# Last expert block turned inside the down product in front, and the sampled tokens' tile taken first in the final combination

## The reference, cut to what matters

```python
h = x + mix
# every token goes to the top 2 of 32 experts; assignments are sorted by expert, padded to blocks of 128 rows
def expert_block(args):
    e, tok = args
    xb = x_pad[tok]
    hmid = jax.nn.silu(xb @ w_gate[e]) * (xb @ w_up[e])
    return hmid @ w_down[e]
out = lax.map(expert_block, (blk_expert, buf_tok.reshape(n_blocks, MOE_BLOCK)))
...
h = h + y                       # y: the two expert rows of a token, each times its gate
y_prompt = rms_norm(yp, norm_final_w)
y_sample = rms_norm(ys, norm_final_w)
```

## Time and profile before

| | us |
|---|---|
| median of 3 runs (1553.66 to 1555.98) | 1553.77 |
| the profiled execution | 1556.07 |
| its span in the trace | 1554.3 |
| TensorE busy | 1434.6 (92%) |
| VectorE busy | 1064.6 (68%) |
| ScalarE busy | 783.2 (50%) |
| GpSimd busy | 554.0 (36%) |

### The profile page before, as it was taken

One profiled execution on the slowest core, in us unless ns is written; L12 is line 12 of the kernel. 1 busy time (PEld: TensorE's weight loads), 2 busy tenths in 40 slices (PEclk: granted clock), 3 DMA queues, 4 the chain that ended last, 5 costly groups with the idle time before them and its releaser, 6 DMA issues. The chain is left out here.

```text
span 1554.3 us, 22508 instructions
## 1 busy us (share of the span) xinstructions
PE 1434.6 (92%) x7643; PEld 1244.0 (80%) x7643; DVE 1064.6 (68%) x1410; ACT 783.2 (50%) x1051; POOL 554.0 (36%) x362
## 2 busy tenths in 40 slices
PE   5999999999999998799998669999999999999955
PEld 3899999989999997688777558788888888888842
DVE  4588723266655655344452659999999999999936
ACT  5342223333334334344343428777787777777714
POOL 5423324454444442584544014423322232221111
PEclk8999999999999999899999669999999999999978
DMA  4123333234444346677453659999999999999867
GB/s 177 42 72 94 112 115 98 78 131 151 149 150 145 136 140 209 230 225 233 157 173 112 223 173 375 384 388 388 380 373 371 383 374 374 376 374 371 308 243 291
DMA packets 166994, 360.58 MB, mean 232 GB/s; under 512 B 20948, under 2 KB 50644, under 8 KB 166932
## 3 DMA queue, kind: packets, MB, share of 16 engines
q1 hardware_dynamic: 151364, 321.85, 58.1%
q0 software_dynamic: 15568, 37.87, 7.2%
HBM read 316.00 MB, written 59.64 MB: 242 GB/s over the span
## 5 line engine op out<-in xcount | busy, mean ns | idle before, releaser
L61 PE MATMUL bank<-xh,wh 128*128 128x352 f32 x864 | 294.9, 341 | 2.9 <-ACT raw L886 2.9
L63 PE MATMUL bank<-xh,wl 128*128 128x352 f32 x864 | 278.8, 323 | 0.0
L62 PE MATMUL bank<-xl,wh 128*128 128x352 f32 x864 | 278.2, 322 | 0.0
L1821 POOL DMA_INDIRECT scratch_picked<-yb,dst x32 | 94.4, 2950 | 246.1 <-DVE yb L1993 246.1
L1906 ACT CAST wg_h<-wg 128x1024 fp32r<-128x1024 f32 x124 | 131.2, 1058 | 96.5 <-PE bank L63 64.6
L1999 DVE TENSOR_TENSOR wg_l<-wg,wg_h 128x1024 fp32r<-128x1024 f32 x128 | 156.2, 1221 | 25.8 <-ACT wu_h L1907 24.3
L61 PEld LDWEIGHTS bank<-xh,wh 128*128 128x128 f32 x864 | 163.2, 189 | 7.3 <-issue 5.5
L1656 POOL TENSOR_TENSOR wol<-wo,woh 128x1024 fp32r<-128x1024 f32 x48 | 120.5, 2522 | 134.2 <-ACT woh L973 134.1
L62 PEld LDWEIGHTS bank<-xl,wh 128*128 128x128 f32 x864 | 163.7, 189 | 2.9 <-issue 1.9
L63 PEld LDWEIGHTS bank<-xh,wl 128*128 128x128 f32 x864 | 162.8, 188 | 0.0
L2000 DVE TENSOR_TENSOR wu_l<-wu,wu_h 128x1024 fp32r<-128x1024 f32 x128 | 155.8, 1217 | 0.0
(11 more groups left out here) (391 smaller groups left out, 3241.2 us busy)
## 6 DMA issues: line engine op xcount, KB each, us to landing
wg<-in_w_gate SPq DMA_DIRECT2D x128, 512.0 KB, 5.8
wu<-in_w_up SPq DMA_DIRECT2D x128, 512.0 KB, 11.1
wd<-in_w_down SPq DMA_DIRECT2D x128, 512.0 KB, 11.4
wo<-in_w_out SPq DMA_DIRECT2D x48, 512.0 KB, 4.7
w<-in_w_in_tiles SPq DMA_DIRECT2D x36, 512.0 KB, 3.7
yy<-scratch_picked SPq DMA_DIRECT2D x8, 1024.0 KB, 13.4
scratch_xb<-stage POOLq DMA_DIRECT2D x10, 512.0 KB, 4.0
xb<-scratch_xb SPq DMA_DIRECT2D x8, 640.0 KB, 4.4
```

The costliest lines, as they stand in the source:

```text
L61: nc.tensor.matmul(acc, lh, rh, start=start, stop=False)
L62: nc.tensor.matmul(acc, lh, rl, start=False, stop=False)
L63: return nc.tensor.matmul(acc, ll, rh, start=False, stop=stop)
L1821: pool.indirect_dma_start(out=S["picked"], out_offset=bass.IndirectOffsetOnAxis(ap=dst[:], axis=0), in_=yb[:], in_offset=None, bounds_chec ...
```

## The change

In `experts`, for the last block only: TensorE turns the hidden rows of m+1 in the middle of `down(m)`, ahead of its third weight piece. The turned rows go to buffers of their own, `last_h` and `last_l`, and the product of m+1 goes to banks 4 and 5, so neither waits for `down(m)` or for y of m. ScalarE casts the turned rows between the second and the third weight piece of m+1, and VectorE makes their low part there and unloads y of m behind it, ahead of the pieces 2 and 3. The last y is copied into `xg`, and its scatter takes its row numbers from `src`, so neither waits for the scatter of m. In `combine`, tile 8 is loaded first, and ScalarE, VectorE and GpSimd take it first (`ORDER`); the semaphores and counts stay as they are.

```diff
+        last_h, last_l = at("last_h", 92160, [P, FF // P, P], F32R), at("last_l", 96256, [P, FF // P, P], F32R)
...
-            scatter(m + 2)
+            last = m + 2
+            then_own(pool, nc.gpsimd.tensor_copy(src[:], of_row[:, 1, bass.ds(last, 1)]), dst_ready, last + 1)
+            pool.wait_ge(y_done, last * 2 + 2)
+            pool.sem_inc(holder, 1)
+            pool.indirect_dma_start(out=S["picked"], out_offset=bass.IndirectOffsetOnAxis(ap=src[:], axis=0),
+                                    in_=xg[:], in_offset=None, bounds_check=2 * T - 1, oob_is_err=False).then_inc(y_stored, 16)
...
-            def down(i):
+            def down(i, first=2, turn_hid_at=None):
                 pe.wait_ge(hT_done, i + 1)
-                wait(pe, y_done, i * 2)
+                parts = (hT_h, hT_l) if first == 2 else (last_h, last_l)
+                wait(pe, y_done, i * 2 if first == 2 else 0)
                 for f in range(FF // P):
+                    if f == turn_hid_at:
+                        turn_hid(i + 1)
                     pe.wait_ge(down_split, i * 4 + (f + 1))
...
-            down(m)
-            turn_hid(m + 1)
-            down(m + 1)
+            down(m, turn_hid_at=2)
+            down(m + 1, first=4)
...
-            high_down(m + 1)
-            high_hid(m + 1)
+            high_down(m + 1, range(2))
+            high_hid(m + 1, last_h)
+            high_down(m + 1, range(2, 4))
...
-            low_down(m + 1)
+            low_down(m + 1, range(2))
+            low_hid(m + 1, (last_h, last_l))
             unload_y(m)
-            low_hid(m + 1)
-            unload_y(m + 1)
+            low_down(m + 1, range(2, 4))
+            dve.wait_ge(down_used, (m + 1) * 4 + 4)
+            for n in range(2):
+                nc.vector.tensor_copy(xg[:, n * 512:(n + 1) * 512], bank[4 + n][:, :]).then_inc(y_done, 1)
...
+ORDER = [8, 0, 1, 2, 3, 4, 5, 6, 7]
...
-            for t in (1, 0, 3, 2, 5, 4, 7, 6, 8):
+            for t in (8, 1, 0, 3, 2, 5, 4, 7, 6):
...
+            add(NT)
             add(0)
-            for t in range(2, NT + 1, 2):
+            norm(NT)
+            for t in range(2, NT, 2):
                 add(t)
                 norm(t - 2)
                 norm(t - 1)
-            norm(NT)
+            norm(NT - 2)
+            norm(NT - 1)
```

More of the change, by code:

```diff
@@ L1869, in down @@
                         s = slice(n * 512, (n + 1) * 512)
-                        last = split_product(nc, bank[2 + n][:, :], (hT_h[:, f, :], hT_l[:, f, :]), (wd_h[:, f, s], wd_l[:, f, s]),
+                        last = split_product(nc, bank[first + n][:, :], (parts[0][:, f, :], parts[1][:, f, :]), (wd_h[:, f, s], wd_l[:, f, s]),
                                              start=(f == 0), stop=(f == FF // P - 1))
@@ L1907, in high_gate_up, with high_down @@
                     nc.scalar.copy(wu_h[:, s, :], wu[:, s, :]).then_inc(gu_high, 1)
-            def high_down(i):
-                for p in range(4):
+            def high_down(i, pieces=range(4)):
+                for p in pieces:
                     act.wait_ge(down_loaded[p], i * 16 + 16)
@@ L1925, in silu, with high_hid @@
                 nc.scalar.activation(act_g[:], bank[0][:, :], ACT.Silu).then_inc(silu_done, 1)
-            def high_hid(i):
+            def high_hid(i, part=hT_h):
                 act.wait_ge(hT_psum, i + 1)
-                wait(act, down_used, i * 4)
-                nc.scalar.copy(hT_h[:], bank[6][:].rearrange("p (k t) -> p k t", k=4)).then_inc(h_high, 1)
+                wait(act, down_used, i * 4 if part is hT_h else 0)
+                nc.scalar.copy(part[:], bank[6][:].rearrange("p (k t) -> p k t", k=4)).then_inc(h_high, 1)
             high_x(0)
@@ L2007, in low_x, with low_down, low_hid @@
                                             xh[:, s, :].bitcast(F32), ALU.subtract).then_inc(xT_done, 1)
-            def low_down(i):
-                for p in range(4):
+            def low_down(i, pieces=range(4)):
+                for p in pieces:
                     dve.wait_ge(down_high, i * 4 + (p + 1))
                     nc.vector.tensor_tensor(wd_l[:, p, :], wd[:, p, :], wd_h[:, p, :].bitcast(F32), ALU.subtract).then_inc(down_split, 1)
-            def low_hid(i):
+            def low_hid(i, parts=(hT_h, hT_l)):
                 dve.wait_ge(h_high, i + 1)
-                nc.vector.tensor_tensor(hT_l[:], bank[6][:].rearrange("p (k t) -> p k t", k=4), hT_h[:].bitcast(F32),
+                nc.vector.tensor_tensor(parts[1][:], bank[6][:].rearrange("p (k t) -> p k t", k=4), parts[0][:].bitcast(F32),
                                         ALU.subtract).then_inc(hT_done, 1)
@@ L2068, in combine @@
         diag_ready, pe_summed = sem("diag_ready"), sem("pe_summed")
-        on_dve = [t for t in range(NT + 1) if t not in ON_PE]
+        on_dve = [t for t in ORDER if t not in ON_PE]
         block = ctx.enter_context(nc.Block())
@@ L2080, in _ @@
         def _(pool):
-            for t in range(NT + 1):
+            for n, t in enumerate(ORDER):
                 r = rows_of(t)
-                pool.wait_ge(out_ready, t + 1)
+                pool.wait_ge(out_ready, n + 1)
                 dst = A["y_sample"] if r == TS else A["y_prompt"][t * P:t * P + r, :]
@@ L2109, in after @@
                 then_own(act, ins, act_own, links[0])
-            for t in range(NT + 1):
+            for t in ORDER:
                 r = rows_of(t)
@@ L2145, in norm @@
                 r = rows_of(t)
-                dve.wait_ge(rms, t + 1)
+                dve.wait_ge(rms, ORDER.index(t) + 1)
                 after(nc.vector.reciprocal(st[0:r, t, 3:4], st[0:r, t, 1:2]))
```

## The result

The changed kernel takes 1563.38 us in the median (8 runs, 1560.42 to 1565.77), the kernel before 1554.88 us beside it. The ratio of the two is 1.0049, 95% interval 1.0037 to 1.0062: it is **slower by 7.6 us** (5.8 to 9.6). The forecast was 3.7 us slower and reached up to 1561.5. The direction and both mechanisms were right; the loss was about twice as large and the time fell outside the range. Of the 5.9 us between 1557.5 and 1563.38, 1.1 us is the base: the forecast was added to 1553.77, the median shown, and the kernel before took 1554.88 in all the runs.

A forecast was written before the change was run, and what follows sets the result against it. It saw an idle TensorE gap and slow clock before the last down product, then the combination's loads and VectorE, as binding. -5.5 + 9.2 = +3.7 us on the 1553.77 median gave 1557.5 us, range 1554.8 to 1561.5.

The forecast's parts named there:

- both mechanisms: Last expert block: idle gap goes, first load 5.5 us earlier; combination: add(8) waits for all loads, 9.2 us more.
- Part 1: Last expert block: the 3.81 us TensorE gap goes, so the combination's first load is issued 5.5 us earlier (4.5 to 6).
- the weight split: Last down product: VectorE's unload waits for a scatter, so weight piece 2 is late and TensorE waits 0.7 us.
- From the last scatter to the first load: End of expert stage: 6.50 us as before, plus 0.3 us for overlap with the scatter ahead (bounds 0 and 1.3).
- part 2: Combination: the shared semaphore holds VectorE's first add until all loads land; first load to end takes 9.2 us more.
- the first root: Combination: norm(8) on VectorE waits 0.3 us for ScalarE's first root, with its table load of 1.28.
- the landing of the last load: Combination: all loads landed 23.2 us behind the first load (22.5 to 25), 0.4 of it for a last landing.
- The bulk: Combination loads: 8.65 MB at an undisturbed rate, without stores beside them, take 22.8 us from the first load.
- B: VectorE's first wait of the combination: the shared count does not hold add(8), giving 1544.9 us; chance 0.03.
- C: Last down product: TensorE's clock falls to 1.2 GHz, +2.5 to +5 us, 1560 to 1562.5; chance 0.10.
- D: Tail: loads finish sooner than 22.8 us or the barrier follows closer than 6.5 us; 1554.5 to 1556.8; chance 0.26.
- two terms that nearly cancel: Whole kernel: first load 5.5 us earlier against a combination 9.2 us longer, net +3.7 us.

The follow-up runs named there:

- e2: The new `combine` alone, with `experts` as before, against the kernel before: ratio 1.0079 (1.0061 to 1.0097), 12.3 us slower.

## Why the prediction was wrong in its size

- **Part 1, step by step: right.** No gap ahead of the last down product, the clock at 1.00, and the weight split as what is late next, with a stop of 1.09 us (0.7 forecast; 0.3 to 0.9 in the other traces). From the last scatter to the first load 6.8 us were forecast and 6.7 to 7.2 measured. Total -5.5 forecast, -4.6 in the profiled execution, -5.1 over all traces, -5.3 timed.
- **The wait in part 2: right.** add(8) at the head of VectorE waited for the last landing. VectorE's work behind it was put at 26.0 us and took 26.05 us; the 0.3 us wait for the first root was there with 0.30.
- **The step that failed: the landing of the last load**, "with 0.4 for a last landing 23.2 us". The bulk was through where it was forecast, 22.7 to 22.9 us behind the first load against 22.8. But the last landing came 25.2 us behind it. The 0.4 is what one landing takes behind its last data (0.43 here), and with it fourteen of the sixteen parts of the last load were in at 23.6. That some parts come late, here by another 1.6 us, was put at nothing, and no row was given for that. The trace of before hid the thin tail in its rates, since stores were under way beside the last loads, but not in its landings: in the fifth to seventh of its loads the last of the sixteen came 2.4 to 2.8 us behind the middle one. With 2.4 in the place of 0.4 the combination costs 11.2 us more, and the sum is -5.5 + 11.2 = 5.7 us; with the 5.1 us that the traces show for part 1 it is 6.1 us, near the 6.6 of the traces and inside the timed interval. The bounds "22.5 and 25" for this term were too tight as well.
- **What is left** between 6.1 and 7.6 is not separated from noise: the interval reaches down to 5.8, and e2 alone measured 12.3 us where its trace shows 11.5 against before.
- **Rivals.** B (the count does not hold add(8)) and C (the clock falls) did not happen. D had the right place, the size of the loads' end, but I had worked it out only towards a smaller loss. That the net stood on two terms that nearly cancel, of which one had a tail that none of the rows shown told of, should have opened the range upwards.

## What to carry to other kernels

When work is moved to the head of an engine's list, look up what else raises the semaphore that it waits for: a count that sums several loads and is waited for in full is only as early as the last of them. A semaphore of its own, or loading its sharer early, turned the change from 7.6 us slower into some 8 us faster than before. When everything waits for the last of many loads, do not take the landing from bytes over rate alone: here 2.2 us of thin tail came behind the bulk. How late the last part of a load lands behind the middle one can be read from the landings of a trace.

## What the runs showed of the hardware

- Behind 8.65 MB of loads without stores beside them the last landing came 2.2 us after the full rate of 406 to 418 GB/s broke off, and the same behind half of the bytes; with the small tile's load last and no stores the tail was 4 us. In the first two about one engine's worth of transfers was left.
- The last of a load's sixteen landings fell further behind the middle one in steps. In nine traces there was a step of 0.7 to 1.5 us in the load under way at an instruction packet of 16 KB, 1.1 us long; that the one causes the other is not shown.
- The first load behind the barrier came 6.5 us after the issue of the last indexed scatter when the scatter before was 9.6 to 10.6 us older (four traces), 6.7 to 7.2 at 5.5 us (five), and 8.3 at 3.2 us (one). From 5.5 to 3.2 us, packing the scatters closer did not bring the barrier forward.
- The start of the last silu varied from 1479.8 to 1485.6 us between single executions of kernels with the same instructions up to there. Spans of two profiled executions cannot be compared to a few us; stretches from a common event can.
